# The two heads of a key/value pair side by side in a window attention, four logits places, and the gated units' mixing at the end of the block

## The reference

```python
q, k, v, ua, va = split_proj(h @ w_in)          # 8 query heads, 2 key/value heads of 64
kc, vc = jnp.split(hc @ w_in[:, Q_W:Q_W + 2 * KV_W], 2, axis=-1)
attn = window_attention(q, k, v, kc, vc, sink)  # 256 own keys within a window, 256 context keys, a sink
mix = chunk_gmlp(ua, va, w_s, b_s)              # gelu, normalise v, mix tokens by w_s, + b_s, times u
y = jnp.concatenate([attn, mix], axis=-1) @ w_out
```

## Time and profile before

| | us |
|---|---|
| runs, median of 3 | 3494.84 (3494.47 to 3500.19) |
| profiled execution, device time | 3459.92 |
| profiled execution, span from first to last instruction | 3458.1 |
| TensorE busy in the span | 2882.1 (83%) |
| VectorE busy | 2255.9 (65%) |
| ScalarE busy | 1300.2 (38%) |
| mean granted TensorE clock, 1 = 2.4 GHz | 0.947 |
| `window_mix`, from its first keep_warm to the first matmul of the next stage | 1847.05 to 1916.34 |
| attention of `finish_mixers`, first logits to first closing keep_warm | 549.36 to 580.02, and 1395.79 to 1426.79 |

### The profile page before, as it was taken

How to read it: one execution, slowest core, us unless ns; L and a number is a source line. 1 busy time by engine, 2 the same in 40 slices (tenths; PEclk the granted TensorE clock), 3 DMA queues, 4 the chain that set the end, 5 groups by cost and what they waited for, 6 DMA issues and landing times. The chain is left out here.

```text
span 3458.1 us, 49482 instructions
## 1 busy us (share of the span) xinstructions
PE 2882.1 (83%) x18504; PEld 2013.2 (58%) x18504; DVE 2255.9 (65%) x4167; ACT 1300.2 (38%) x2831; POOL 586.8 (17%) x516
## 2 busy tenths in 40 slices
PE   7999888899999988889769777777777667777776
PEld 7987786797988788589647652232322642223232
DVE  6666665676865766566554567777775577777774
ACT  4343324433433432443224334444443234444443
POOL 0000000000000000000000034444443034444442
PEclk9999999999999999999879889999999889999999
DMA  7665101566764500255641269999998469999997
GB/s 273 219 209 164 47 3 62 195 231 248 248 246 151 171 11 3 110 199 203 264 187 68 69 241 425 426 425 425 425 423 355 139 279 425 425 425 425 425 425 301
DMA packets 251784, 864.00 MB, mean 250 GB/s; under 512 B 14896, under 2 KB 138928, under 8 KB 178736
## 3 DMA queue, kind: packets, MB, share of 16 engines
q0 software_dynamic: 73728, 536.90, 37.0%
q1 hardware_dynamic: 177840, 324.31, 26.9%
HBM read 852.77 MB, written 8.39 MB: 249 GB/s over the span
## 5 line engine op out<-in xcount | busy, mean ns | idle before, releaser
L2509 POOL DMA_INDIRECT raw_weights<-peer_rows,expert_ids x208 | 237.2, 1140 | 2431.3 <-DVE expert_ids L148 2167.8
L778 DVE TENSOR_TENSOR weight_parts_lo<-raw_weights,weight_parts_hi 128x2048 fp32r<-128x2048 f32 (+7 forms) x202 | 433.6, 2172 | 164.4 <-ACT weight_parts_hi L747 164.4
L2597 PE MATMUL banks<-raw_weights,diagonals 128*128 128x512 f32 x832 | 402.7, 624 | 140.7 <-ACT diagonals L181 140.4
L2597 PE MATMUL banks<-expert_rows,diagonals 128*128 128x512 f32 x816 | 398.4, 627 | 115.9 <-ACT diagonals L181 115.0
L447 PE MATMUL banks<-normedT_hi,weight_parts_hi 128*128 128x256 f32 x1664 | 474.1, 285 | 17.7 <-DVE weight_parts_lo L778 9.5
L747 ACT CAST weight_parts_hi<-raw_weights 128x2048 fp32r<-128x2048 f32 (+7 forms) x202 | 358.3, 1810 | 305.5 <-PE banks L449 255.7
L448 PE MATMUL banks<-normedT_lo,weight_parts_hi 128*128 128x256 f32 x1664 | 471.9, 284 | 0.0
L449 PE MATMUL banks<-normedT_hi,weight_parts_lo 128*128 128x256 f32 x1664 | 471.6, 283 | 0.0
L2597 PEld LDWEIGHTS banks<-raw_weights,diagonals 128*128 128x128 f32 x832 | 152.4, 195 | 387.5 <-ACT diagonals L181 214.4
L2597 PEld LDWEIGHTS banks<-expert_rows,diagonals 128*128 128x128 f32 x816 | 149.5, 195 | 362.8 <-ACT diagonals L181 232.6
L181 ACT ACTIVATE gelu<-dots 128x1 f32<-128x1 f32 x512 | 103.5, 202 | 655.8 <-DVE dots L157 655.1
(11 more groups left out here) (394 smaller groups left out, 5035.0 us busy)
## 6 DMA issues: line engine op xcount, KB each, us to landing
raw_weights<-ffn_in SPq DMA_DIRECT2D x88, 1024.0 KB, 7.4
side_weights<-mod_tiles SPq DMA_DIRECT2D x48, 1024.0 KB, 5.5
raw_weights<-ffn_out SPq DMA_DIRECT2D x44, 1024.0 KB, 7.0
raw_weights<-w_in SPq DMA_DIRECT2D x28, 1024.0 KB, 5.0
raw_weights<-peer_w_q SPq DMA_DIRECT2D x16, 1024.0 KB, 5.1
raw_weights<-w_in SPq DMA_DIRECT2D x10, 1536.0 KB, 6.6
raw_weights<-w_branch SPq DMA_DIRECT2D x8, 1024.0 KB, 7.3
raw_weights<-w_out SPq DMA_DIRECT2D x8, 1024.0 KB, 6.7
```

The source lines that it names most:

```text
L778: nc.vector.tensor_tensor(parts.lo[:, u, cs], raw[:, cs], parts.hi[:, u, cs].bitcast(F32), ALU.subtract).then_inc(low, 1)
L2509: nc.gpsimd.indirect_dma_start(out=ring[r], out_offset=None, in_=table, in_offset=bass.IndirectOffsetOnAxis(ap=ids[:, n, t:t + 1], axis=0) ...
L2597: last = nc.tensor.matmul(k.bank(2 * j + half), diag[:, g % DIAGS, :], ring[g % RING][:, D + half * BANK:D + (half + 1) * BANK], start=t = ...
```

## The change

Three edits in `window_mix` and one in `finish_mixers`.

1. `finish_mixers`, `logits(n)`: both bias matmuls come first, then both q times k matmuls.
2. `window_mix`: logits are made for a pair at a time: context keys for e = 0 and e = 1, own keys for e = 0 and e = 1, then the two masks. `lg` and the logits banks have four places in place of three. TensorE makes pairs 0 and 2 in front of the loop, and pair n+2 in each even n.
3. `window_mix`: two more `keep_warm` matmuls stand in front of the wait for the q and k copies, and two more behind the first two pairs.
4. `window_mix`: `mixing(0)` and `mixing(1)` both stand in the last turn of the loop, behind turn(15) and in front of values(14), into banks 0 and 1; the gates follow store(14) and store(15), and the semaphore `unit_made` is gone.

```diff
                     for mm in range(2):
                         nc.tensor.matmul(spot(n)[:, mm, :], C("ident"), alibi[:, j, h, :], start=True, stop=False)
+                    for mm in range(2):
                         ks = slice(mm * HA, mm * HA + HA)
...
-        lg = k.sb("logits", [P, 3, 2 * SEQ], ctx=c)
+        lg = k.sb("logits", [P, 4, 2 * SEQ], ctx=c)
...
-                def logits(n):
-                    e, q, j = units[n]
-                    if n >= 3:
+                def pair_logits(n):
+                    _, q, j = units[n]
+                    if n >= 4:
                         pe.wait_ge(S["exped"], 2 * (n - 3) + 1)
-                    ks = slice(e * 64, e * 64 + 64)
-                    nc.tensor.matmul(k.bank(n % 3)[:, SEQ:], qT[ks, j, q, :], kT[ks, SEQ:], start=True, stop=True)
-                    nc.tensor.matmul(k.bank(n % 3)[:, 0:SEQ], qT[ks, j, q, :], kT[ks, 0:SEQ], start=True, stop=False)
-                    nc.tensor.matmul(k.bank(n % 3)[:, 0:SEQ], C("ident"), room.window[:, j, :],
-                                     start=False, stop=True).then_inc(S["summed"], 1)
+                    half = lambda e: slice(e * 64, e * 64 + 64)
+                    for e in range(2):
+                        nc.tensor.matmul(k.bank((n + e) % 4)[:, SEQ:], qT[half(e), j, q, :], kT[half(e), SEQ:],
+                                         start=True, stop=True)
+                    for e in range(2):
+                        nc.tensor.matmul(k.bank((n + e) % 4)[:, 0:SEQ], qT[half(e), j, q, :], kT[half(e), 0:SEQ],
+                                         start=True, stop=False)
+                    for e in range(2):
+                        nc.tensor.matmul(k.bank((n + e) % 4)[:, 0:SEQ], C("ident"), room.window[:, j, :],
+                                         start=False, stop=True).then_inc(S["summed"], 1)
...
                 def mixing(j):
                     pe.wait_ge(S["v_normed"], j + 1)
-                    if j:
-                        pe.wait_ge(S["unit_made"], j)
                     for g in range(GROUPS):
-                        last = nc.tensor.matmul(k.bank(3)[:, g * 64:g * 64 + 64], room.spatialT[:, g, :],
+                        last = nc.tensor.matmul(k.bank(j)[:, g * 64:g * 64 + 64], room.spatialT[:, g, :],
...
+                keep_warm(k, 3, 2)
                 pe.wait_ge(S["qk_out"], NT + 1)
-                for n in range(2):
-                    logits(n)
+                pair_logits(0)
+                pair_logits(2)
+                keep_warm(k, 7, 2)
                 for n in range(N + 1):
-                    if n + 2 < N:
-                        logits(n + 2)
+                    if n % 2 == 0 and 4 <= n + 2 < N:
+                        pair_logits(n + 2)
                     if n < N:
                         turn(n)
+                    if n == N - 1:
+                        for j in range(NT):
+                            mixing(j)
                     if n >= 1:
                         values(n - 1)
-                    if n == 12:
-                        mixing(0)
-                mixing(1)
...
-                    if n >= 3:
-                        act.wait_ge(S["turned"], n - 2)
                     if n >= 4:
+                        act.wait_ge(S["turned"], n - 3)
                         act.wait_ge(S["stored"], n - 3)
...
-                    elif n == 14:
+                    elif n >= N:
                         dve.wait_ge(S["gelued"], 2 * NT)
-                        gate(0)
-                gate(1)
+                        gate(n - N)
```

More of the change, by code:

```diff
@@ L2119, in turn @@
                         last = nc.tensor.transpose(k.bank(4 + n % 2)[:, kc * P:kc * P + P],
-                                                   lg[:, n % 3, kc * P:kc * P + P], C("ident"))
+                                                   lg[:, n % 4, kc * P:kc * P + P], C("ident"))
                     last.then_inc(S["turned"], 1)
@@ L2177, in exps @@
                     act.wait_ge(S["masked"], n + 1)
-                    if n >= 3:
-                        act.wait_ge(S["turned"], n - 2)
                     if n >= 4:
+                        act.wait_ge(S["turned"], n - 3)
                         act.wait_ge(S["stored"], n - 3)
-                    o.fn(lg[:, n % 3], k.bank(n % 3), ACT.Exp, bias=mx[:, n % 4:n % 4 + 1],
+                    o.fn(lg[:, n % 4], k.bank(n % 4), ACT.Exp, bias=mx[:, n % 4:n % 4 + 1],
                          total=sm[:, n % 4, 0:1], free=True).then_inc(S["exped"], 1)
@@ L2237, in masks @@
                     dve.wait_ge(S["summed"], n + 1)
-                    o.max(mx[:, n % 4:n % 4 + 1], k.bank(n % 3), free=True)
+                    o.max(mx[:, n % 4:n % 4 + 1], k.bank(n % 4), free=True)
                     o.ts(mx[:, n % 4:n % 4 + 1], mx[:, n % 4:n % 4 + 1], room.sink[:, h:h + 1], ALU.max,
@@ L2274, in gate @@
                         cs = slice(g * 64, g * 64 + 64)
-                        last = o.stt(mix[:, j, QW + g * 64:QW + g * 64 + 64], k.bank(3)[:, cs], room.biasT[:, g:g + 1],
+                        o.stt(mix[:, j, QW + g * 64:QW + g * 64 + 64], k.bank(j)[:, cs], room.biasT[:, g:g + 1],
                                      u[:, j, cs], ALU.add, ALU.mult, free=True)
-                    last.then_inc(S["unit_made"], 1)
                 for j in range(NT):
@@ L2617 @@
               + ["lam_exped", "qk_turned", "qk_out", "state_made", "state_kept", "y_whole", "y_squared", "y_varied",
-                 "y_rooted", "y_shifted", "y_normed", "out_squared", "roped", "gelued", "v_normed", "units_mixed", "unit_made"]
+                 "y_rooted", "y_shifted", "y_normed", "out_squared", "roped", "gelued", "v_normed", "units_mixed"]
               + ["high", "low"] + [f"{e}_lane{g}" for e in ("pe", "act", "dve") for g in range(2)])
```

## The result

| | before | after |
|---|---|---|
| runs of the first comparison, median of 4 each, us | 3494.65 (3469.12 to 3500.19) | 3450.15 (3445.42 to 3452.14) |
| profiled execution, us | 3459.92 | 3452.14 |
| `window_mix`, first keep_warm to the next stage's first matmul, in that profile | 69.29 | 55.80 |
| `finish_mixers`, its state matmuls (L1742) to the next stage, layers 1 and 2 | 43.59, 43.46 | 41.46, 41.37 |

The changed kernel is faster, ratio 0.9885 with a 95% interval of 0.9835 to 0.9934. A second comparison with 12 executions of the changed kernel and 29 of the kernel before gave 0.9924 (0.989 to 0.9959).

What follows compares the result with a forecast made beforehand. TensorE was taken to bound `window_mix`, with TensorE and ScalarE both nearly full in `finish_mixers`. Terms of -13.5 and -4.2 gave -17.7 us, 3459.9 to 3442.2 profiled; with 34.9 carried over, 3477 us, 8 in 10 range 3469 to 3487.

Steps and rivals of the forecast that it cites:

- Packed halves -7.0: `window_mix`: a pair's four q times k matmuls cost two, 0.436 us less per unit, 16 units, -7.0 us.
- fewer changes of rows -3.2: `window_mix`: two changes between 64-row and 128-row matmuls per pair, no longer four, 0.20 us per unit, -3.2 us.
- The rival that the halves don't run at once: Both stages: only changes of rows are saved, -8.5 us in all, 3486 us; chance 0.06.
- The smaller gain, by some 2.4 us: `window_mix`: at the skill's efficiency two tiles give 1.5 times, so the gain would be some 2.4 us smaller.
- Keep_warm in front +0.6, behind +1.7: `window_mix`: added keep_warm costs 0.6 us before the first logits, partly inside the gap, and 1.7 behind the first pairs.
- Mixing +1.6: End of `window_mix`: with both mixings behind turn(15), the way to the next stage takes 10.0 against 8.4 us, +1.6.
- new waits +0.8: `window_mix`: TensorE's unit falls to 2.33 us, close to VectorE's 2.27; new waits cost 0 to +3, taken +0.8.
- First part -2.1 per layer: `finish_mixers`: ScalarE sets the pace, so only start and end gain, -2.1 us per layer, -4.2 in both.
- The rival that TensorE is the bound there: `finish_mixers`: TensorE alone sets the pace, gain 13.1 us in place of 4.2, whole 3468 us; chance 0.05.
- Clock -8.0: `window_mix`: the half-speed stretch goes and its 17.0 us of work take 9.0, -8.0 us, bounds 0 and -8.0.
- The median lies 34.9 above the profiled execution: Whole kernel: this difference is carried over, taking the forecast from 3442.2 us profiled to 3477 us measured.
- rival 5: Elsewhere in the kernel: half-clock stretches fall differently and eat 10 us of the gain, 3488 us; chance 0.05.

Runs made afterwards that it cites:

- e4: Changed kernel with packing undone, each head's three matmuls in a row: `window_mix` 65.20 us against 55.80, whole 3462.19 us in one run.
- e7: Changed kernel without the two keep_warm matmuls behind the first pairs: `window_mix` 54.07 us, median 3447.23 us.
- e6: Changed kernel without its four added keep_warm matmuls: `window_mix` 53.55 us, median 3448.62 us.
- e5: Kernel before plus two keep_warm matmuls in front of the wait for the q and k copies: `window_mix` 61.82 us, median 3456.06 us.
- e3: Kernel before with only the `finish_mixers` edit: ratio 0.9998 (0.9958 to 1.0037), median 3490.80 us, `window_mix` 104.85 us.
- e1: Kernel before, unchanged, run again beside itself: median 3493.09 us, `window_mix` 101.23 us.
- e2: Changed kernel, unchanged, run again on one chip with the kernel before: ratio 0.9924, median 3451.27 us, `window_mix` 55.80 us.
- e9: Changed kernel without any keep_warm in `window_mix`, the six old ones included: 48.41 us from first logits, median 3450.93 us.
- e12: Changed kernel with heads' matmuls unpacked and without the four added keep_warm: `window_mix` 67.36 us, median 3459.39 us.
- e11: Changed kernel with the logits ordered context e0, own e0, context e1, own e1: `window_mix` 55.84 us, whole 3445.26 us in one run.

## Why the prediction was wrong

**The direction and the work saved in the stages were right; the size of the clock term and the carrying to the median were not, and the first part's gain did not reach the whole.** Point by point:

- *Packed halves -7.0, fewer changes of rows -3.2.* e4 against the changed kernel: 9.4 of 10.2. Right, for the two together. The rival that the halves don't run at once is out, and L1068 was the right row for it. A pair's logits cost 2.03 us (1869.25 to 1871.28), close to the 2.14 of full overlap. The smaller gain, by some 2.4 us, that was estimated from the 3.07 times for four row tiles in the Trainium skill, "TensorE: Matmul & The Clock Gate", section "Why this matters for your kernels", is not seen in it: by that estimate a pair would cost about 2.4 us.
- *Keep_warm in front +0.6, behind +1.7.* 0.52 (e7 less e6) and 1.73. Right.
- *Mixing +1.6, new waits +0.8.* Not measured one by one. e5 against e7, which differ in packing, places and mixing, gives -7.75 where the terms sum to -7.0 - 3.2 + 1.6 + 0.8 = -7.8.
- *First part -2.1 per layer.* Right in the stage, and wrong for the whole: the sum let everything behind the layer move up with it, and in most profiles the next stage took about 2 us more (e3). The rival that TensorE is the bound there is out.
- *Clock -8.0.* **This is the step that failed.** "If the half-speed stretch goes, its 17.0 us of work" took the length of the stretch in one profile as the kernel's. It is no property of the kernel but of the execution: 17.1 us there, 85.3 and 95.1 in the two other profiles of the same list. That the change would end the stretch was right, for a reason that the sum named (gap filled, half rows made whole); each of the two alone would have done (e5, e6). Against e1 the term is 101.23 + 0.52 - 61.82 = 39.9 us, five times the 8.0. The bound "0 and -8.0" was drawn round one reading.
- *"The median lies 34.9 above the profiled execution, and I carry the difference over."* The second half of the same fault. A gap of 1% between a profile and the runs of the same kernel was a sign that this profile was of another kind than they, and the half-clock stretch with a busy TensorE was the place to look: the whole of the units at half clock costs about 15 x 2.63 = 39 us, of which the profile showed 8, and the missing 31 are most of the 34.9. Had I worked that out, the forecast would have been some 3446, 4 us under the measured median; that it would be so near is partly luck, for it leaves out the 7 us of the next paragraph.

The sum in the trace of e1 and e2, both from the same chip, is: `window_mix` -45.4, `finish_mixers` -4.0, and +7 in stages that the change does not touch, together -42.4 (3489.7 to 3447.2). Of these 7, 2.4 lie ahead of layer 1, where nothing differs in the lists, 1.7 between the two layers, 2.3 between layer 2 and `window_mix` and the rest behind it. In the first pair of profiles it was 9.9. My rival 5 had this, 10 us, at a chance of 0.05, and it came in both pairs. It also means that the forecast for the profiled execution itself, 3442.2, missed: 3452.14 was measured. The two faults have opposite signs: between e1 and e2 the forecast had 32 us of gain too little in `window_mix`, and 7 too much elsewhere. And the 0.2% that a measurement of this kernel was said to tell was too hopeful: with the base's scatter e3's interval is 0.4% to either side.

The rival on the slow side (packed stages lose the clock) went the other way round: it was the unpacked stage that could not keep it.

## What to carry to other kernels

When the runs of a kernel lie a per cent above its profile, the profile may show a lucky execution: find the stretch in which it could have been unlucky (TensorE busy, PEclk 0.50), and price it at its full length before anything else. Here a stage whose matmuls partly use half the rows, entered behind a wait of 1.12 us, stayed at half clock to its end in one profile (e3) and for 17 us in another; two matmuls on constants in front, or running the two halves side by side, took away both the half clock and the scatter. Between two profiles the two matmuls were worth 39 us; by the medians they were worth 24, and the whole change 43 on another chip, for the chips differ in how often the kernel before is unlucky. A gain that is real in its stage can be given back by the next one (e3): read both. Compare kernels stage by stage in the profiles and by many executions in the whole; neither alone told the story here.

## What the runs showed of the hardware that was not expected

- TensorE at 1.2 GHz and busy all the time did not come back to 2.4 GHz for 85.3 us (e1), while the packed order, begun at 1.2 GHz, came back 5.7 us after its first logits (e9). The unpacked order by pairs came back after 10.2 us (e12).
- After a wait of 1.12 us in front of the logits the clock fell 2.3 us into them with unpacked halves behind it (e1, e12), and not with packed halves (e6) or with the wait filled by two matmuls (e5).
- The stage behind layer 1 takes 41.4 to 41.5 us to a later matmul when the clock falls 0.5 to 0.8 us after its start, and 43.4 to 43.8 when it fell before (all 14 profiles).
- Matmuls on different halves overlap across the list, past one that waits for its own half (e11: 55.84 us against 55.80, the two starts 0.01 us apart).
